# Dilated keys of a hybrid decoder layer: three weight units as seven block products instead of eight, VectorE making the first unit's weight sums

## The reference

```
h = rmsnorm(x, norm_mix[l])
proj = h @ w_in[l]
q_a, kv_a, g_a, qkv_b, g_m = jnp.split(proj, IN_SPLITS, axis=-1)
...
y_a = nsa_attention(q_a, kv_a, g_a, ...)
qkv_b = qkv_b.reshape(B, S, 3, len(DIL_GROUPS), DIL_HPG, HEAD_DIM)
for gidx, (window, dil) in enumerate(DIL_GROUPS):
    o_g, lse_g = dilated_group(qkv_b[:, :, 0, gidx], qkv_b[:, :, 1, gidx],
                               qkv_b[:, :, 2, gidx], window, dil, slopes_dil[gidx])
...
x = x + (merged @ w_out[l])
gt, up = jnp.split(rmsnorm(x, norm_ffn[l]) @ w_ffn_in[l], 2, axis=-1)
x = x + (silu(gt) * up) @ w_ffn_out[l]
return rmsnorm(x, norm_final)
```

## Time and profile before

| | before |
|---|---|
| three runs, us | 772.27, 772.29, 774.03; median 772.29 |
| the profiled execution, us | 774.13 |
| its span (first to last instruction), us | 772.3 |
| PE busy | 761.0 us, 99% of the span, 5498 matmuls |
| DVE busy | 547.4 us, 71% |
| ACT busy | 358.4 us, 46% |
| POOL busy | 153.8 us, 20% |
| granted PE clock, mean | 0.997 |
| HBM read, written | 77.44 MB, 5.29 MB |

### The profile page before, as it was taken

How to read it: one execution, slowest core, us unless ns; L and a number is a source line. 1 busy time by engine, 2 the same in 40 slices (tenths; PEclk the granted TensorE clock), 3 DMA queues, 4 the chain that set the end, 5 groups by cost and what they waited for, 6 DMA issues and landing times.

```text
span 772.3 us, 13726 instructions
## 1 busy us (share of the span) xinstructions
PE 761.0 (99%) x5498; PEld 683.7 (89%) x5498; DVE 547.4 (71%) x1026; ACT 358.4 (46%) x674; POOL 153.8 (20%) x122
## 2 busy tenths in 40 slices
...
GB/s 219 335 166 55 109 56 164 58 130 42 105 61 56 56 56 1 42 42 190 118 155 55 164 109 66 125 123 124 112 109 109 110 83 63 105 107 157 173 108 109
DMA packets 104637, 83.59 MB, mean 108 GB/s; under 512 B 16976, under 2 KB 94848, under 8 KB 104576
## 3 DMA queue, kind: packets, MB, share of 16 engines
...
...
HBM read 77.44 MB, written 5.29 MB: 107 GB/s over the span
## 4 chain that ended last, share of the span: by engine, by line
PE 93%; DVE 3%; ACT 2%; POOL 1%; issue 1%; DMA 0%; ACTq 0%; DVEq 0%; POOLq 0%
PE bank L1938 24%; PE bank L1940 24%; PE bank L1939 24%; PE bank L2171 3%; PE bank L2190 2%; PE bank L2420 2%; PE bank L2419 2%; PE bank L2418 2%; PE bank L2158 2%; PE bank L2072 1%; PE bank L2113 1%; PE bank L2094 1%; PE bank L2035 1%; ACT h_hi L958 1%; ACT t_sums L950 1%
## 5 line engine op out<-in xcount | busy, mean ns | idle before, releaser
L1196 DVE TENSOR_TENSOR w_lo<-w_raw,w_hi 128x2048 fp32r<-128x2048 f32 (+2 forms) x29 | 64.5, 2224 | 79.5 <-ACT w_hi L752 79.5
L1938 PE MATMUL bank<-n_hi,w_hi 128*128 128x512 f32 x272 | 108.8, 400 | 0.0
L1940 PE MATMUL bank<-n_hi,w_lo 128*128 128x512 f32 x272 | 106.1, 390 | 0.0
L1939 PE MATMUL bank<-n_lo,w_hi 128*128 128x512 f32 x272 | 106.0, 390 | 0.0
L752 ACT CAST w_hi<-w_raw 128x2048 fp32r<-128x2048 f32 (+2 forms) x29 | 53.6, 1848 | 61.8 <-PE bank L1940 51.2
L713 POOL TENSOR_TENSOR n_lo<-merge_tmp,n_hi 128x512 fp32r<-128x512 f32 x8 | 10.4, 1299 | 298.2 <-ACT n_hi L934 298.2
L1654 DVE TENSOR_TENSOR sums_lo<-weight_sums,sums_hi 128x1024 fp32r<-128x1024 f32 x38 | 64.4, 1736 | 0.3 <-ACT sums_hi L994 0.3
L1938 PE MATMUL bank<-t_hi,sums_hi 128*128 128x256 f32 x228 | 63.0, 276 | 1.1 <-ACT m_u_u L1002 1.1
L1939 PE MATMUL bank<-t_lo,sums_hi 128*128 128x256 f32 x228 | 62.9, 276 | 0.0
L1940 PE MATMUL bank<-t_hi,sums_lo 128*128 128x256 f32 x228 | 62.9, 276 | 0.0
L1938 PE MATMUL bank<-w_hi,n_hi 128*128 128x256 f32 (+2 forms) x192 | 62.1, 323 | 0.0
...
## 6 DMA issues: line engine op xcount, KB each, us to landing
w_raw<-in_w_ffn_in_dram SPq DMA_DIRECT2D x44, 512.0 KB, 5.0
w_raw<-in_w_in_dram SPq DMA_DIRECT2D x37, 512.0 KB, 4.7
w_raw<-in_w_ffn_out_dram SPq DMA_DIRECT2D x22, 512.0 KB, 3.5
w_raw<-in_w_out_dram SPq DMA_DIRECT2D x8, 512.0 KB, 4.0
...
xs<-in_x_dram SPq DMA_DIRECT2D x4, 512.0 KB, 5.1
...
```

The costliest lines, as they stand in the source:

```text
L1196: dve.tensor_tensor(wlo[u % 2][:, split_part(u)], raw[u % 2][:, 0:n], whi[u % 2][:, split_part(u)].bitcast(F32), ALU.subtract).then_inc(lo ...
L1938: pe.matmul(dst, w[0], x_[0], start=start, stop=False)
L1939: pe.matmul(dst, w[0], x_[1], start=False, stop=False)
L1940: return pe.matmul(dst, w[1], x_[0], start=False, stop=stop)
```

## The change

The three key units are no longer six tiles but three jobs `keys(u)`, each of seven block products of 12 matmuls with 256 moving columns (`block_product`). In the order of issue they are: P1 and P2 with plain weights and plain input, P3 with a plain weight block and input sum 3, P4 with weight sum 1 and input sum 1, P5 with weight sum 0 and input sum 0, P6 with weight sum 2 and input sum 2, P7 with weight sum 3 and plain input.

The input sums `n_mixed` (four, of 128x1024) are made once, by 10 DVE instructions during the query units; ACT makes their high parts, DVE their low parts in the order 3, 1, 0, 2 (`t_lo` counts them). The weight sums of unit 4 are made by DVE (`key_weight_sums`, four instructions of 128x512), those of units 5 and 6 by POOL (`weight_sums`), which starts when `t_lo` is 3. `wk_hi` and `wk_lo` are the parts of the plain blocks. `keys_out` adds the shared products and scales the result into `kb`. `dil_bias` moves from `cmp_hidden` into `keys(6)`, `cmp_bias` and `nsa_bias` from `cmp_kv` behind the work of `dil_scores(0)`. `vc` moves to another address, the first two value tiles to PSUM banks 2 and 3, and the counts of the feed-forward units are shifted by those of the key units.

```diff
+KEY_UNITS = (4, 5, 6)
...
-    jobs += [("tile", n) for n in range(FIRST_TILE[U_KB], FIRST_TILE[U_KB + 1])]
-    jobs.append(("cmp_kv", 0))
-    jobs += [("tile", n) for n in range(FIRST_TILE[U_KB + 1], FIRST_TILE[U_VB])]
+    jobs += [("keys", U_KB), ("cmp_kv", 0), ("keys", U_KB + 1), ("keys", U_KB + 2)]
...
+        elif job == "keys":
+            load(n + 2)
...
+    def weight_sums(u, k, full, w, used):
+
+        s = u % 2
+        pool.wait_ge(*full)
+        for b, (a0, a1, op) in enumerate(((w[:, 0:4, P:256], w[:, 4:8, P:256], ALU.add),
+                                          (s7[s][:, 0], w[:, 0:4, 0:P], ALU.subtract),
+                                          (w[:, 0:4, 0:P], w[:, 0:4, P:256], ALU.subtract),
+                                          (w[:, 4:8, 0:P], s7[s][:, 1], ALU.subtract))):
+            if used[b]:
+                pool.wait_ge(*used[b])
+            if b in (1, 3):
+                pool.wait_ge(s_sums, 4 * k + (1 if b == 1 else 2))
+            pool.tensor_tensor(s7[s][:, b], a0, a1, op).then_inc(s_sums, 1)
+
+    pool.wait_ge(blk_same, 2)
+    pool.wait_ge(t_lo, 3)
+    for u in KEY_UNITS[1:]:
+        if u - 2 in KEY_UNITS:
+            used = [(m_done, 7 * (u - 2 - U_KB) + v) for v in (5, 5, 6, 7)]
+        else:
+            used = [unit_used(u - 2), None, None, None]
+        weight_sums(u, u - U_KB, (raw_full[u % 2], raw_count(u)), slot_view(raw, u, KC, 256), used)
...
+        if u + 1 == U_KB:
+            if a == 0:
+                key_plain_hi(U_KB, 0)
+                for v in (2, 1, 3):
+                    key_mixed_hi(v)
+                key_sums_hi(U_KB)
+            else:
+                key_plain_hi(U_KB, 1)
+                key_mixed_hi(0)
...
+    def key_sums_hi(u):
+        s = u % 2
+        act.wait_ge(s_sums, 4 * (u - U_KB) + 4)
+        act.wait_ge(*unit_used(u - 2))
+        for half in range(2):
+            pair = slice(2 * half, 2 * half + 2)
+            act.copy(shi7[s][:, pair], s7[s][:, pair]).then_inc(hi_done if half else s_hi, 1)
+
+    def keys(u):
+        k = u - U_KB
+        act.wait_ge(m_done, 7 * k + 1)
+        if k:
+            act.wait_ge(u2_made, k)
+            act.wait_ge(g_sums, k)
+        act.copy(key_m1u4u3[:, 0, :], ps[TILE_BANK[FIRST_TILE[u]] + 1][:, 0:256]).then_inc(m1_out, 1)
+        if u + 1 in KEY_UNITS:
+            key_plain_hi(u + 1, 0)
+            key_plain_hi(u + 1, 1)
+            key_sums_hi(u + 1)
+        else:
+            split_hi(u + 1)
...
+            if n == FIRST_TILE[U_QB + 1]:
+                key_mixed(2)
+            elif n == LAST_TILE[U_QB + 1]:
+                key_mixed(1)
+                key_mixed(3)
+            elif n == FIRST_TILE[U_QB + 2]:
+                key_weight_sums()
+                key_mixed(0)
+            elif n == LAST_TILE[U_QB + 2]:
+                key_sums_lo(U_KB, 0)
+                key_mixed_lo(0)
+                key_sums_lo(U_KB, 1)
+                key_mixed_lo(2)
...
+    def key_mixed(b):
+        dst = nt[b][:]
+        if b == 2:
+            link(dve.tensor_tensor(dst, n_f[:, second, late], n_f[:, first, late], ALU.subtract))
+            link(dve.tensor_tensor(dst, dst, n_l[:, second, late], ALU.add))
+            last = dve.tensor_tensor(dst, dst, n_l[:, first, late], ALU.subtract)
...
+    def key_weight_sums():
+
+        w = slot_view(raw, U_KB, KC, 256)
+        sums = s7[U_KB % 2]
+        dve.wait_ge(raw_full[U_KB % 2], raw_count(U_KB))
+        dve.wait_ge(*unit_used(U_KB - 2))
+        dve.tensor_tensor(sums[:, 0], w[:, 0:4, P:256], w[:, 4:8, P:256], ALU.add).then_inc(s_sums, 1)
+        dve.tensor_tensor(sums[:, 2], w[:, 0:4, 0:P], w[:, 0:4, P:256], ALU.subtract).then_inc(s_sums, 1)
+        dve.wait_ge(s_sums, 1)
+        dve.tensor_tensor(sums[:, 1], sums[:, 0], w[:, 0:4, 0:P], ALU.subtract).then_inc(s_sums, 1)
+        dve.wait_ge(s_sums, 3)
+        dve.tensor_tensor(sums[:, 3], w[:, 4:8, 0:P], sums[:, 1], ALU.subtract).then_inc(s_sums, 1)
+
+    def key_sums_lo(u, half):
+        s, pair = u % 2, slice(2 * half, 2 * half + 2)
+        if half:
+            dve.wait_ge(hi_done, u + 1)
+        else:
+            dve.wait_ge(s_hi, u - U_KB + 1)
+        dve.tensor_tensor(slo7[s][:, pair], s7[s][:, pair], shi7[s][:, pair].bitcast(F32),
+                          ALU.subtract).then_inc(lo_done if half else s_lo, 1)
...
+    def keys_out(u):
+
+        k, a = u - U_KB, TILE_BANK[FIRST_TILE[u]]
+        dve.wait_ge(u4u3_made, k + 1)
+        dve.wait_ge(m_done, 7 * k + 7)
+        for part in range(2):
+            bank = ps[a][:] if part == 0 else twin[a // 2 + 1].rearrange("p b c -> p (b c)")[:, 256:768]
+            added = key_m1u4u3[:, 0:2, :] if part == 0 else key_m1u4u3[:, 2:3, :].to_broadcast([P, 2, 256])
+            done = up_sums if part else g_sums
+            dve.tensor_tensor(pair_of(bank), pair_of(bank), added, ALU.add).then_inc(done, 1)
+            dve.wait_ge(done, k + 1)
+            dst, src, row = of_group(kb, k, part, bank, rrow[:])
+            dve.scalar_tensor_tensor(out=dst, in0=src, scalar=1.0, in1=row,
+                                     op0=ALU.mult, op1=ALU.mult).then_inc(tile_evac_dve, 1)
+
+    def keys(u):
+        k, a, more = u - U_KB, TILE_BANK[FIRST_TILE[u]], u + 1 in KEY_UNITS
+        if k:
+            keys_out(u - 1)
+        if not more:
+            dil_bias()
+        if more:
+            key_plain_lo(u + 1, 0)
+            key_plain_lo(u + 1, 1)
+        dve.wait_ge(m1_out, k + 1)
+        dve.wait_ge(m_done, 7 * k + 4)
+        dve.tensor_tensor(key_u2[:], ps[a + 1][:, 256:512], key_m1u4u3[:, 0, :], ALU.add).then_inc(u2_made, 1)
+        if more:
+            key_sums_lo(u + 1, 0)
+            key_sums_lo(u + 1, 1)
+        else:
+            split_lo(u + 1)
+        dve.wait_ge(u2_made, k + 1)
+        dve.wait_ge(m_done, 7 * k + 6)
+        if k:
+            dve.wait_ge(up_sums, k)
+        dve.tensor_tensor(key_m1u4u3[:, 1:3, :], pair_of(ps[a + 3][:]),
+                          key_u2[:].unsqueeze(1).to_broadcast([P, 2, 256]), ALU.add).then_inc(u4u3_made, 1)
+        if not more:
+            keys_out(u)
...
-        dil_bias()
+        key_plain_lo(U_KB, 0)
+        key_mixed_lo(3)
+        key_plain_lo(U_KB, 1)
+        key_mixed_lo(1)
...
-        cmp_bias()
-        nsa_bias(0)
...
+            if n == 0:
+                cmp_bias()
+                nsa_bias(0)
...
+    def block_product(dst, w, x_):
+
+        for j in range(4):
+            ins = split_product(dst, [v[:, j, :] for v in w], [v[:, j, :] for v in x_], j == 0, j == 3)
+        ins.then_inc(m_done, 1)
...
+        if u - 2 in KEY_UNITS:
+            tile_evacuated(LAST_TILE[u - 2])
+        else:
+            pe.wait_ge(cmp_tile_evac, 2)
+        pe.wait_ge(wa_lo, 2 * k + 1)
+        block_product(ps[a + 1][:, 0:256], plain(0, 4), x1)
+        block_product(ps[a][:, 0:256], plain(4, 8), x2_)
+        if k == 0:
+            tile_evacuated(LAST_TILE[U_KB - 1] - 1)
+            pe.wait_ge(t_lo, 1)
+        elif k == 1:
+            pe.wait_ge(kv_evac, 2)
+        pe.wait_ge(wa_lo, 2 * k + 2)
+        block_product(ps[a + 2][:, 256:512], [v[s][1] for v in (khi7, klo7)], mixed(3))
+        pe.wait_ge(s_lo, k + 1)
+        pe.wait_ge(m1_out, k + 1)
+        if k == 0:
+            pe.wait_ge(t_lo, 2)
+        block_product(ps[a + 1][:, 256:512], summed(1), mixed(1))
+        if k == 0:
+            tile_evacuated(LAST_TILE[U_KB - 1])
+            pe.wait_ge(t_lo, 3)
+        block_product(ps[a + 3][:, 0:256], summed(0), mixed(0))
+        if k == 0:
+            pe.wait_ge(t_lo, 4)
+        pe.wait_ge(hi_done, u + 1)
+        pe.wait_ge(lo_done, u + 1)
+        block_product(ps[a + 3][:, 256:512], summed(2), mixed(2))
+        block_product(ps[a][:, 256:512], summed(3), x3_)
```

More of the change, by code:

```diff
@@ L105, in sevens, with ready_count @@
 def sevens(u):
-    return sum(v < u for v in SEVEN)
+    return NK + sum(v < u for v in SEVEN)
 def plains(u):
-    return u - sevens(u)
+    return u - sum(v < u for v in SEVEN)
+def ready_count(n):
+    return n - 1 - (2 * NK if n > LAST_TILE[KEY_UNITS[-1]] else 0)
 def out_sevens(n):
@@ L873, in _ @@
                     tile(n)
+                elif job == "keys":
+                    keys(n)
                 elif job == "cmp_hidden":
@@ L1368, in tile, with of_group @@
                         ins.then_inc(blk_cross, 1)
+            def of_group(to, g, a, src, row):
+                dst = to[:, 2 * g + a, :]
+                if g:
+                    dst = dst.rearrange("p (r t) -> p r t", r=4)
+                    src, row = (v.rearrange("p (t r) -> p r t", r=4) for v in (src, row))
+                return dst, src, row
+            early, late = slice(0, 256), slice(256, 512)
+            first, second = slice(0, 4), slice(4, 8)
+            n_f, n_l = nhi[:].bitcast(F32), nlo[:].bitcast(F32)
@@ new lines, in key_mixed @@
+            def key_mixed(b):
[4 more added lines that the diff above has]
```

(13 more changed lines are left out.)

126 lines of the change are left out of this document (83 added, 43 removed).

## The result

| | before | after |
|---|---|---|
| six runs each, us | 772.27 to 774.03, median 772.69 | 775.22 to 777.42, median 775.95 |
| the profiled execution, us | 774.13 | 777.42 |
| its span | 772.3 | 775.6 |
| granted PE clock, mean | 0.997 | 0.994 |

The ratio of after to before is 1.0036, with a 95% interval of 1.0026 to 1.0047. The kernel became 3.3 us slower. The forecast was 772.9 us with a range up to 775.2, so the result lies outside.

What follows compares the result with a forecast made beforehand. PE, 93% of the chain that ended last, was taken to bound the kernel. -4.1 (PE's work) + 0.1 (P6) + 3.9 (P3) + 0.6 (value tile) = +0.5 us, taken as +0.6: 772.9 us, range 769.8 to 775.2.

Steps and rivals of the forecast that it cites:

- What PE saves: Key stage: 252 matmuls at 0.1133 us take 28.6 us plus three starts, instead of 33.0 us; saving 4.1 us.
- The chain behind the low parts: From `t_lo` 3 at 66.8 us, POOL, ACT and DVE's `vc` hold P3 of unit 5 until 80.9: 3.9 us wait.
- POOL's, 7.9 us: POOL's four weight sums of unit 5, slowed by DVE beside them: 7.9 us, lower bound 5.2 us.
- The value tile: First value tile waits for DVE's low part of unit 7 until 99.0 us: 0.6 us.
- the clock: Rival: PE's clock falls in the wait of unit 5, matmuls behind it run at half rate; 774.7 to 776.4 us, chance 0.12.
- The sum: Whole kernel: saving, two waits in the keys and one at the value tile give +0.5 us, taken as +0.6: 772.9 us.
- the idleness in that row, 3.6 us: End of the earlier kernel: granted clock fell from 2.4 to 1.2 GHz after PE idled 3.6 us; used as the clock's condition.
- the signs of being wrong that I had named: POOL done by 72.5, no PE idleness near 77, other matmul interval, PE waits before 70, or clock below 1.00 at 77-90 us.
- "slower": Chance of a time above 774.6 us: 0.15, from the clock rival and half of the DVE lateness rival.
- the gain shows: Rival: POOL and DVE hinder each other less, P3 of unit 5 waits less; 769.0 us fully, 771.0 halfway, chance 0.16.
- DVE's lateness goes on into the value tiles: Rival: unit 8's low part or the bank of `keys_out` is late too; 774 to 775 us, chance 0.10.
- the margins of about a microsecond: Behind the first value tile: bank of `keys_out` and unit 8's low part fit by about 1 us, costed at nothing.

Runs made afterwards that it cites:

- the kernel without waits: The changed kernel with DVE's order mended, half of `dil_bias` and `nsa_bias(0)` later, and two places for m1 and the shared sums: 769.61 us, ratio to before 0.9955.
- results and `cmp_kv` first: The changed kernel with the shared sum, `keys_out(4)` and `cmp_kv` ahead of the low parts of unit 5's sums on DVE: 773.55 us, ratio to before 1.0005.
- Filling the wait: The changed kernel with 36 unused matmuls on PE between P2 of unit 5 and its wait for `kv_evac`: 774.03 us, ratio to before 1.0016.
- the middle start: The changed kernel with POOL's sums waiting for `s_lo` 1 in place of `t_lo` 3: 774.76 us, ratio to before 1.0024.
- the mended orders: The changed kernel with results and `cmp_kv` first on DVE, 773.55 us; the same with `dil_bias` also behind `keys_out(6)`, 771.29 us.
- POOL later: The changed kernel with POOL's sums waiting for `wa_lo` 4 in place of `t_lo` 3: 776.86 us, ratio to before 1.0050.
- half filled: The changed kernel with 18 unused matmuls on PE ahead of P3 of unit 5: 774.88 us, ratio to before 1.0020.
- `cmp_kv` first: The changed kernel with DVE's copies `kc` and `vc` ahead of the low parts of unit 5's weight sums: 775.98 us, ratio to before 1.0029.
- POOL early: The changed kernel with POOL's sums waiting for `s_sums` 4 in place of `t_lo` 3: 771.73 us, ratio to before 0.9990.

## Why the prediction was wrong

**What PE saves** was right in its mechanism, and a little large: 4.1 us forecast, 3.9 measured in the kernel without waits. Twelve matmuls of a product took 1.36 us, as in the feed-forward unit; units 4, 5 and 6 took 9.68, 9.77 and 9.66 us against 9.62.

**The chain behind the low parts** was right in place, releaser and order, and off by 0.8 us in size. Shifted by the 1.96 us by which this execution was earlier, PE was to stop at 75.0 (it did at 75.1), and P3 was to start at 78.9 (79.74). The wait measured 4.7 instead of 3.9 us. The term that was mis-sized here is POOL's, 7.9 us from the earlier trace rows, measured 8.85: one sum held for 5.03 us and three at 1.3, instead of four at 2. The rest of the chain was right: the low parts took 3.43 us against 3.45.

**The value tile** was to wait 0.6 us for the low part of unit 7 and did not. DVE ended it at 98.99 us, but PE came to it only at 99.43, since its products had run at half rate. With the clock restored and the key stage short, this wait came back: 2.0 us in the kernel with results and `cmp_kv` first.

**The step that failed is the clock**, in "The rivals" and in "The sum". I wrote "It decides when the wait is as long as the idleness in that row, 3.6 us; for a shorter one no row shows a fall", gave this rival 0.12, and left the clock out of the sum. My forecast of the wait, 3.9 us, already met that condition, so by my own working it was the likelier case and not one in eight. With the 2.1 us that the clock cost, the sum would have been 775.0 instead of 772.9 us. The longer wait (0.8), the smaller saving (0.2), the value tile that did not wait (-0.6) and a median of the kernel before that came out 0.4 us higher over six runs make up nearly all of what is left to 775.95. Of the signs of being wrong that I had named, it was the granted clock below 1.00 that came. (The chances of "slower", 0.12 and half of 0.10, make 0.17 and not 0.15; that changes nothing.) The row was also a poor bound. It is one observation at the end of the program. In the runs the clock fell about 2.1 us after PE had stopped (after), and idle stretches of 2.7, 2.9 and 2.0 us were enough, the last two with the fall after PE was back at work. The price in the rival, 1.8 to 3.5 us, held the measured 2.1, and its 774.7 to 776.4 us hold the result.

The ledger of the key stage then closes: -3.9 (PE's work) + 4.7 (wait) + 2.1 (clock) = +2.9 us, and the positions gave +2.94. Filling the wait takes 1.4 to 1.9 us off, which shows most of the clock's part; the kernel that removes the waits takes all of it off and more, which shows that the rest was the wait.

The rival *the gain shows* asked for a lucky interleaving of POOL and DVE. The held sum went against it, and if they had taken turns, as in the middle start, DVE's own low parts would have come late in turn. *DVE's lateness goes on into the value tiles* did not take place in after. It did in two of the mended orders (2.0 us at unit 7, 0.9 at unit 8), so the margins of about a microsecond that I cost at nothing were real.

The Trainium skill, page "TensorE: Matmul & The Clock Gate", section "HAM oscillation — how this bites in real kernels", which the prediction set beside this rival, says that a wait between groups of matmuls makes the next group start cold. These traces agree for the waits of 4.9, 4.7, 4.1 and 2.7 us: P3 behind the wait took 2.7 us instead of 1.36 (after, POOL later, half filled), and with `cmp_kv` first P4 started at half rate. Behind the waits of 2.9 and 2.0 us the next group started at full rate and lost it about a microsecond later, and behind the wait of 2.2 us in the kernel with POOL early it kept it.
